# Relative bias of the MoBA scores added by VectorE from a skewed table, and two heads' scores ahead of the last mixer tile

## The reference

```python
own_pos = q_blk * BLK + blk_ar
bias_own = rel_bias[:, rel_bucket(q_pos[:, None] - own_pos[None, :])]
s_own = jnp.einsum('bhqd,bhkd->bhqk', q_c, k_own).astype(f32) + bias_own.astype(f32)[None]
s_own = jnp.where(own_pos[None, :] <= q_pos[:, None], s_own, -jnp.inf)
...
probs = jax.nn.softmax(logits, axis=-1).astype(v.dtype)
```

## Time and profile before

| what | us |
|---|---|
| three timed executions | 2479.95, 2473.61, 2477.56 |
| their median | 2477.56 |
| profiled execution, first to last instruction (span) | 2475.7 |
| median less that span | 1.9 |
| TensorE busy in the span | 2411.7 (97%) |
| VectorE busy | 1606.0 (65%) |
| ScalarE busy | 1033.3 (42%) |
| mean granted clock of TensorE | 0.994 of full speed |

### The profile page before, as it was taken

How to read it: one execution, slowest core, us unless ns; L and a number is a source line. 1 busy time by engine, 2 the same in 40 slices (tenths; PEclk the granted TensorE clock), 3 DMA queues, 4 the chain that set the end, 5 groups by cost and what they waited for, 6 DMA issues and landing times. The chain is left out here.

```text
span 2475.7 us, 41693 instructions
## 1 busy us (share of the span) xinstructions
PE 2411.7 (97%) x17447; PEld 2055.0 (83%) x17447; DVE 1606.0 (65%) x2242; ACT 1033.3 (42%) x1365; POOL 99.2 (4%) x179
## 2 busy tenths in 40 slices
PE   7999999999999999999999999999999999998999
PEld 7999989999999999899999854464888887647999
DVE  6887756778888887657798632671744442474555
ACT  5445534454554455335454321661422222263333
POOL 2010000001101100000001000000000000000000
PEclk9999999999999999999999999999999999999999
DMA  8776503647777775116467742102532331212452
GB/s 283 251 271 216 168 3 120 205 145 267 252 254 239 272 244 160 46 54 213 162 229 255 272 155 68 52 2 71 167 102 90 98 102 52 81 56 69 162 195 69
DMA packets 270807, 381.97 MB, mean 154 GB/s; under 512 B 9593, under 2 KB 235209, under 8 KB 268994
## 3 DMA queue, kind: packets, MB, share of 16 engines
q1 hardware_dynamic: 251628, 314.47, 38.7%
q0 software_dynamic: 18128, 64.20, 7.2%
q10 hardware_dynamic: 902, 1.15, 0.2%
HBM read 366.13 MB, written 13.65 MB: 153 GB/s over the span
## 5 line engine op out<-in xcount | busy, mean ns | idle before, releaser
L704 PE MATMUL ps<-span 128*128 128x512 f32 x1280 | 453.9, 399 | 2.3 <-issue 1.2
L635 PE MATMUL ps<-span,w_low 128*128 128x256 f32 x1440 | 408.0, 283 | 0.0
L706 PE MATMUL ps<-span,w_low 128*128 128x256 f32 x1280 | 359.5, 281 | 0.0
L633 PE MATMUL ps<-span 128*128 128x256 f32 x1216 | 348.6, 287 | 8.2 <-DVE span L1585 5.2
L1603 DVE TENSOR_TENSOR w_low<-ring,span 128x2048 fp32r<-128x2048 f32 x131 | 299.8, 2288 | 82.3 <-ACT span L1267 82.3
L1267 ACT ACTIVATE span<-ring 128x2048 fp32r<-128x2048 f32 x131 | 250.6, 1915 | 135.5 <-DMA ring<-in_ffn_w_in 112.8
L704 PEld LDWEIGHTS ps<-span 128*128 128x128 f32 x1280 | 240.6, 188 | 60.3 <-issue 1.3
L635 PEld LDWEIGHTS ps<-span,w_low 128*128 128x128 f32 x1440 | 277.0, 192 | 0.0
L634 PE MATMUL ps<-span 128*128 128x256 f32 x864 | 245.3, 284 | 0.0
L633 PEld LDWEIGHTS ps<-span 128*128 128x128 f32 x1216 | 233.8, 192 | 12.4 <-DVE w_low L1603 5.4
L706 PEld LDWEIGHTS ps<-span,w_low 128*128 128x128 f32 x1280 | 241.9, 189 | 0.0
(11 more groups left out here) (487 smaller groups left out, 5337.3 us busy)
## 6 DMA issues: line engine op xcount, KB each, us to landing
ring<-in_ffn_w_in SPq DMA_DIRECT2D x88, 1024.0 KB, 8.9
ring<-in_w_mlp SPq DMA_DIRECT2D x64, 1024.0 KB, 5.3
wmod<-in_w_mod POOLq DMA_DIRECT2D x96, 512.0 KB, 6.8
ring<-in_ffn_w_out SPq DMA_DIRECT2D x44, 1024.0 KB, 5.2
ring<-in_w_mix_in SPq DMA_DIRECT2D x26, 1024.0 KB, 5.5
ring<-in_xattn_w_kv SPq DMA_DIRECT2D x16, 1024.0 KB, 5.4
mod_scratch<-mod_acc POOLq DMA_DIRECT2D x24, 512.0 KB, 6.2
ring<-mod_scratch SPq DMA_DIRECT2D x12, 1024.0 KB, 4.9
```

Of the source, the lines that this page charges most:

```text
L633: mm(dst, w_hi, x_hi, start=start, stop=False, **more)
L635: return mm(dst, w_lo, x_hi, start=False, stop=stop, **more)
L704: mm(ps[bank + m].rearrange("p (w t) -> p w t", w=2), hi[:, k, cols], span[:, :, k, :], start=(k == 0), stop=False, skip_group_check=True)
L706: last = mm(ps[bank + m][:, 0:T], lo[:, k, cols], h_high[:, k, :], start=False, stop=(k == KD - 1), skip_group_check=True)
```

## The change

It has three parts.

1. The bias leaves TensorE. L793, L795 and the constant `flip` are gone. `maxima(h)` is given the bias table and uses `tensor_tensor_reduce`: it adds the table to the scores in place in PSUM and keeps the largest sum. The exponentials read the same bank as before.
2. The table is `toep`, whose partition p is the row read backwards from `hank`'s start. GpSimd writes the 8 rows to memory 16 times (one DMA, 128 rows of 512), and reads the table with eight DMAs of 16 partitions.
3. The scores use the banks `MOBA_BANKS = (2, 3, 0, 1, 4, 5, 0, 1)`. Heads 0 and 1 are scored right behind the head sums, ahead of the last mixer tile. ScalarE's exponentials of heads 0 and 1 stand ahead of its copy of the last tile, with a wait for the end of that tile in front of them. The scores of a head now wait for an earlier head's exponentials from head 6 on.

```diff
 def scores(h):
-    pair, hb, bank = h // 2, (h % 2) * HD, ps[SCORE_BANKS[h % 4]]
-    if h >= 4:
+    pair, hb, bank = h // 2, (h % 2) * HD, ps[MOBA_BANKS[h]]
+    if h >= 6:
         pe.wait_ge(*sm_act.at(l, 2 * (h - 3)))
     hi = slice(hb, hb + HD)
-    mm(bank[:, 0:T], cst["flip"], hank[:, h, :], start=True, stop=False, ...)
-    mm(bank[:, T:T + P], cst["flip"], hank[:, h, P:T], start=False, stop=False, ...)
-    mm(bank[:, 0:T], mq[hi, pair, P:T], mk[hi, pair, :], start=False, stop=False, ...)
-    mm(bank[:, T:T + P], mq[hi, pair, 0:P], mk[hi, pair, 0:P], start=False, stop=True, ...)
+    mm(bank[:, 0:T], mq[hi, pair, P:T], mk[hi, pair, :], start=True, stop=True)
+    mm(bank[:, T:T + P], mq[hi, pair, 0:P], mk[hi, pair, 0:P], start=True, stop=True
+       ).then_inc(*sc_done.up())
...
+def attend(first, end):
+    if first == 0:
+        pe.wait_ge(*mix_evac.at(l, 10))
+        pe.wait_ge(*act_step.at(l, ACT_KK_STD))
+    else:
+        pe.wait_ge(*dve_step.at(l, DVE_FEATURES))
+        pe.wait_ge(*mix_evac.at(l, MIX_TILES - 1))
+    for h in range(first, end):
+        step(h)
...
                     head_sums(tmp, 0)
-            pe.wait_ge(*dve_step.at(l, DVE_FEATURES))
-            moba(l)
+                    attend = moba(l)
+                    attend(0, 2)
+            attend(2, NH + 3)
...
 # GpSimd
-pool.dma_start(scratch["bias"], bias_rows).then_inc(bias_stored.sem, 16)
+pool.dma_start(scratch["bias"], bias_rows.rearrange("h (o t) -> h o t", o=1).to_broadcast(
+    [NH, BIAS_ROWS, 2 * T])).then_inc(bias_stored.sem, 16)
 pool.wait_ge(bias_stored.sem, 16)
-pool.dma_start(hank[:, :, :], bass.AP(src.tensor, 0, [[1, P], [2 * T, NH], [1, T]])
+for p in range(0, P, BIAS_ROWS):
+    pool.dma_start(toep[p:p + BIAS_ROWS, :, :], bass.AP(
+        src.tensor, P - 1 - p, [[2 * T - 1, BIAS_ROWS], [BIAS_ROWS * 2 * T, NH], [1, T]])
...
 # ScalarE, in front of take() of a value tile
+if n == MIX_TILES - 1:
+    act.wait_ge(w_used[FIRST_AT[("mix_in", j)] % RING].sem, freed(FIRST_AT[("mix_in", j)], l) + 1)
+    exponential, turned = softmax(l, 0, 1.0, (T, P), MOBA_BANKS)
+    exponential(0)
+    exponential(1)
 take(l, ("mix_in", j), mix_bank(n), mv[:, :, (j - 11) * BLK:(j - 10) * BLK], mix_evac)
...
 # VectorE, maxima(h)
-v.tensor_reduce(smx[:, e, t:t + 1], ps[banks[e]][:, at:at + w], AX_X, ALU.max
-                ).then_inc(*sm_max.up())
+if biases:
+    v.tensor_tensor_reduce(bank[:, at:at + w], bank[:, at:at + w], biases(h, t), 1.0,
+                           -3.0e38, ALU.add, ALU.max, smx[:, e, t:t + 1]).then_inc(*sm_max.up())
```

More of the change, by code:

```diff
@@ L113, in constants @@
         "head_ones": f(r // HD == c // HD),
-        "flip": f(r + c == P - 1),
         "eye": f(j == t),
@@ L164 @@
 SCORE_BANKS = (0, 1, 4, 5)
+MOBA_BANKS = (2, 3, 0, 1, 4, 5, 0, 1)
+BIAS_ROWS = 16
+BIAS_READY = 16 + P // BIAS_ROWS * 16
 CROSS_BANKS = (0, 1, 5, 4)
@@ L270, in program @@
         store["v_loaded"] = [Signal(ctx, nc, f"v_loaded{s}") for s in range(RING2)]
-        scratch = {"bias": nc.dram_tensor("bias_scratch", (NH, 2 * T), F32).ap(),
+        scratch = {"bias": nc.dram_tensor("bias_scratch", (NH, BIAS_ROWS, 2 * T), F32).ap(),
                    "mod": nc.dram_tensor("mod_scratch", (DEPTH, P, 2, MODS * P), F32).ap()}
@@ L312, in build_first @@
         part("under_mem", [P, KD, T])
-        part("under_hank", [P, NH, T])
+        part("under_toep", [P, NH, T])
         g_low = part("g_low", [P, KD, T])
@@ L335, in build_first @@
     mem_sb = sb("mem_sb", [P, KD, T])
-    hank = sb("hank", [P, NH, T])
+    toep = sb("toep", [P, NH, T])
     mix_buf = sb("mix_buf", [P, RAW + 4 * T])
@@ L820, in out, with step @@
                 last.then_inc(*av_done.up())
[L822 to L825, removed]
+            def attend(first, end):
[7 more added lines that the diff above has]
+                    step(h)
+            def step(h):
                 if h < NH:
@@ L831, in moba @@
                     out(h - 3)
+            return attend
         def heads_of(e):
@@ L1344, in exponential @@
             def exponential(h):
-                e, g, bank = h % 4, base + h, ps[banks[h % 4]]
+                e, g, bank = h % 4, base + h, ps[banks[h % len(banks)]]
                 act.wait_ge(*sm_max.at(l, 3 * (g + 1)))
@@ L1469, in scalar_program @@
             col_high(l, KV0)
-            exponential, turned = softmax(l, 0, 1.0, (T, P), SCORE_BANKS)
-            for h in range(NH + 2):
+            for h in range(2, NH + 2):
                 if h < NH:
@@ L1751, in shift, with softmax @@
                                                b[:, m, 1:T + 1], ALU.mult, ALU.add), mixed)
-        def softmax(l, base, scale, widths, banks):
+        def softmax(l, base, scale, widths, banks, biases=None):
             def maxima(h):
-                e, g = h % 4, base + h
+                e, g, bank = h % 4, base + h, ps[banks[h % len(banks)]]
                 dve.wait_ge(*sc_done.at(l, g + 1))
@@ L1758, in maxima @@
                 for t, w in enumerate(widths):
-                    v.tensor_reduce(smx[:, e, t:t + 1], ps[banks[e]][:, at:at + w], AX_X, ALU.max
-                                    ).then_inc(*sm_max.up())
+                    if biases:
+                        v.tensor_tensor_reduce(bank[:, at:at + w], bank[:, at:at + w], biases(h, t), 1.0,
+                                               -3.0e38, ALU.add, ALU.max, smx[:, e, t:t + 1]).then_inc(*sm_max.up())
+                    else:
+                        v.tensor_reduce(smx[:, e, t:t + 1], bank[:, at:at + w], AX_X, ALU.max
+                                        ).then_inc(*sm_max.up())
                     at += w
@@ L1969, in vector_program @@
             step(l, v.memset(state[:, :, :], 0.0), seq_step)
-            maxima, weights = softmax(l, 0, 1.0, (T, P), SCORE_BANKS)
+            if l == 0:
+                dve.wait_ge(bias_stored.sem, BIAS_READY)
+            maxima, weights = softmax(l, 0, 1.0, (T, P), MOBA_BANKS, lambda h, t: toep[:, h, t * P:T])
             evac = moba_out(l)
```

2 lines of the change are left out of this document (1 added, 1 removed).

## The result

The changed kernel takes 2488.2 us (median of four executions, 2483.65 to 2489.97) against 2478.8 us for the kernel before on the same chip (four, 2473.61 to 2481.05). The ratio is 1.0043, 95% interval 1.0029 to 1.0057: it is slower by 0.43% (the two medians alone give 1.0038). The forecast was 2472.5 us, and 2481 at most.

The account below looks back on a forecast made before the run. TensorE, busy 97% of the span, was taken as the bound. Per layer 6.80 us of products plus 1.37 of old waits less 5.6 of new gave 2.6, 5.1 in both: 2475.7 - 5.1 = 2470.6, median 2472.5; range 2467 to 2481.

Parts of the forecast that it names:

- TensorE's clock falls in the new gap: Rival: behind the idle 2.4 us before head 2 the clock drops, costing 1.6 us a layer, 2475.7 in all; chance 0.08.
- Bias products off TensorE, 6.80 a layer: Attention on TensorE: eight heads each lose 0.85 us of bias products, 6.80 us a layer, all in the gapless stretch.
- Two heads ahead of the last tile, 1.70 us, "no work is saved": Heads 0 and 1 scored before the last mixer tile: the tile starts 1.70 us later and ends at 303.95.
- Early scores gain nothing, head 2 waits 2.4: TensorE idles 2.4 us before head 2, which starts at 306.3 against 306.35 before; only heads 2 to 7 collect, 5.1.
- The pair at 0.95: VectorE's two sum-with-maximum instructions for a head, start to start up to the negation: 0.95 us, between 0.81 and 1.14.
- pipelined case: VectorE's pair with each accumulator read adding only 0.08 us: 0.81 us, a gain of 3.3 us a layer.
- cheap pair's rival: Rival: VectorE's pair costs as little as the reductions, 0.65 to 0.75 us; 7.0 to 7.8 gained, 2470.2; chance 0.2.
- New waits behind: TensorE waits appearing after head 2 starts, before the transposes of heads 1, 3 and 6: 0.8, 1.15 and 0.7 us.
- Edits at nothing: ScalarE's weight tile, GpSimd's eight table reads (up to 7.5 us to issue), SP's later loads and the shorter constants' load: no cost.
- Behind the attention "the gain is kept": After the attention TensorE's list keeps its order and the loads follow, so the 2.6 us a layer survives.
- VectorE as the bound: Rival: the pair takes 1.84 us in all 16 heads and every transpose waits; +1.9 us a layer, 2481.4; chance 0.12.

Follow-up runs that it names:

- e2: Kernel before with only the new banks and order, heads 0 and 1 scored early, bias products kept on TensorE: 2488.12 us, ratio 1.0051.
- e11: Kernel before with one unread product in front of TensorE's wait for the last mixer tile's copy: 2475.67 us, ratio 0.9996.
- e9: Changed kernel with four unread products of 64 rows filling TensorE's gap in front of head 2: 2473.55 us, ratio 0.9995.
- e3: Changed kernel with ScalarE's copy of the last mixer tile moved ahead of the exponentials of heads 0 and 1: 2483.25 us, ratio 1.003.
- e4: Changed kernel with four unread products of 128x128 by 128x256 in TensorE's gap in front of head 2: 2473.52 us, ratio 0.9997.
- e8: e1 with three unread products of 64 rows and 128 columns ahead of each head's scores: 2476.88 us, ratio 0.9999.
- e6: e5 with two unread products, one before the wait for the last tile's copy, one before head 0's transposes: 2467.95 us, ratio 0.9965.
- e5: e3 with both halves of the next projection's first weight tile made earlier, on ScalarE and VectorE: 2478.27 us, ratio 1.0011.
- e1: Changed kernel with the old order and banks, so only the bias moves to VectorE: 2487.07 us, ratio 1.0044.
- e10: e6 with a third unread product, in front of the wait for head 6's weights: 2467.48 us, ratio 0.9964.

## Why the prediction was wrong

**The step that failed** is the rival "TensorE's clock falls in the new gap". The prediction named the mechanism and its place, and sized both numbers wrongly: a chance of 0.08 and a price of "0.41 x 4 = 1.6 us" a layer.

- *The price.* It was the cost of the stretch in which the earlier trace rows show a clock of 0.59, as if a fall always ended after 4 us. Behind the attention's gap the clock was down for some 20 us. From head 2 to the last copy that is 24.50 - 17.68 = 6.8 us a layer and not 1.6. What should have been asked is what all the work behind the gap costs at half clock, up to the end of the attention: a head without its bias takes 2.13 at full clock and took 3.88, so five heads are 8.75 more, less the waits of 1.6 us (0.36, 0.69, 0.52) that vanish beside so slow an engine: 7.2 by this estimate, 6.8 measured.
- *The chance.* The argument against was that "TensorE is dense up to the 2.4 us gap here, and fairly dense behind it". The trace before had a counterexample: the stretch of the earlier trace rows lies behind an idle time of just this length. Of the kernel before:

```profile
1453.26 0.42 PE L2526 MATMUL ps<-consts_sb,sqm 24*128 24x24 f32 x4 [0.84 <-DVE sqm L3163]
1456.14 8.37 PE L2705 MATMUL ps<-h_sb,ring 128*128 128x512 f32 x15 [2.45 <-ACT h_sb L2919]
```

  The prediction called this "a thin stretch with gaps" and did not set the length of the gap beside its own. A wait of 2.45 us is followed by a fall there, 0.6 us behind its end; a forecast wait of 2.4 us should have been given the same, with a chance over a half. Not certainty: in the same trace a wait of 2.76 us, up to 2284.57, kept the full clock, and in the twelve profiles together the wait of 2.45 goes with a fall in ten and not in e2 and e11. That the fall was short there (0.98 from 1460 on) and long here is shown but not explained: there TensorE ran full-array products of 512 columns, here short products, transposes and outputs. e2 and e9 only say that the count of rows is not what decides whether it falls.

The Trainium skill, TensorE: Matmul & The Clock Gate, "Why this matters for your kernels", advises against idle gaps between bursts of products because one takes the clock to its lower level, but it names only gaps longer than any forecast here. The traces agree that idle time brings the clock down and differ on how much it takes: 2.39 us in one piece, and in e3 0.78 and 0.61 in two, were enough, and the measurement decides.

**The other steps, in order.**

- *Bias products off TensorE, 6.80 a layer*: right. They are gone, and e4, at full clock, gains 3.75 us up to the first layer's last copy.
- *Two heads ahead of the last tile, 1.70 us, "no work is saved"*: wrong, to the change's favour. The two took 0.86 us together, side by side, and the tile ended 0.6 us sooner than forecast.
- *Early scores gain nothing, head 2 waits 2.4*: the wait is right, 2.39, released by the copy of `mv`. Head 2 is at 305.74 where 306.3 was forecast and 306.35 stood before, so the early scores gained 0.6 us after all.
- *The pair at 0.95*: 0.78. The main parts are 0.43 and 0.33 (0.42 and 0.28 were taken); of the two reads of 0.14 only the second costs anything, 0.11. By the prediction's own scale this is just under its pipelined case, 0.81, and just over the cheap pair's rival (0.65 to 0.75).
- *New waits behind*: with the pair at 0.78 they are smaller, as e4 shows: 0.36 in front of head 1's transposes (forecast 0.8), 0.69 at head 3's (1.15), 0.52 at head 6's (0.7). Their order, with head 3 behind `col_low` the longest, was right. In the changed kernel itself they vanish, since TensorE at half speed waits for nobody.
- *Edits at nothing*: right for the features (+0.10). GpSimd's eight reads take 4.21 us of issuing, under the 7.5 allowed; the last goes out 71 us before the table is used.
- *Behind the attention "the gain is kept"*: off by 1.44 in the first layer and 0.48 in the second, where the recurrence is longer, with TensorE idle 0.84 in front of L878:

```profile
344.89 0.81 PE L878 MATMUL ps<-sc,mk 64*64 64x64 f32 x18 [0.84 <-issue]
```

  From the last copy of `cat` to the recurrence's first sum into it the first layer takes 31.82 us before, 33.26 after, and in the other kernels 31.84 (e2), 31.93 (e8), 32.48 (e11), 32.65 (e4), 32.70 (e6), 32.72 (e3), 32.78 (e5), 33.01 (e9), 33.28 (e1), 33.47 (e10). That follows neither the order nor the bias nor the clock of the attention. TensorE waits there for nothing that the profile records; what it is stays open, at some 2 us of the whole.
- *VectorE as the bound*: did not come. VectorE is idle in front of five of the eight maxima of the first layer, and in e4, at full clock, still in front of three.

The forecast time was the sum of steps that were mostly right or priced too high, the recurrences apart, at a clock that the change itself takes away.

## What to carry to other kernels

Taking work off a dense engine is only a gain if no idle stretch takes its place at a spot where much short work follows: list every wait of TensorE that the change will leave, and where they are like those here, price all the work behind them at half clock. Read the clock column beside the busy share, and look in the trace before for a wait of the same length and what the clock did after it. When such a wait can't be closed, two to four cheap products that nobody reads, in front of it, are worth trying; and what feeds the waiting instruction (here a weight tile's two halves) can be moved ahead of it. And where two heads of 64 rows lie on different halves of the partitions, score them back to back with nothing of full height between: here the second one cost nothing.

## What the hardware did that was not expected

- A fall of the clock outlasts its cause by far. In the changed kernel, e1, e2 and e3 there are eight such stretches in the attention, two in each; seven last 20 to 24 us, one (e2's second layer) 7, nearly all of it with TensorE recorded as busy. In the kernel before, behind 2.45 us of idle, it was under 4. What ends such a stretch stays open.
- The edge is soft. The second block, the same program in all twelve profiles, has waits of TensorE that can be counted: a stretch at the lower clock begins in the wait or up to 2.1 us behind it in none of the twelve at the wait of 1.74 us, in two at 1.77, in nine at 2.17, in ten at 2.45, in nine at 2.76 and in all at 4.00. e5's two layers have the same waits to 0.01 us, and one kept the clock and the other lost it; a median over a dozen executions then lies between two kinds of execution, and one profile shows only one of them.
- Products of 64 rows on partitions 0 to 63 and on 64 to 127 run side by side when they follow each other directly: two heads' scores take 0.86 us together in the changed kernel and 0.73 in e1 (303.29 to 304.02), with one head at 0.85. In e8 dummies on partitions 0 to 63 stand in line with head 0's scores (304.03, then 304.15) and run beside head 1's (305.02 and 305.03). In the kernel before, with bias products of 128 rows between them, each head's took its full 0.85 (303.80 to 304.65, 305.50 to 306.35).
- VectorE's read of the accumulator, 0.14 us long, starts at the same time as the instruction behind it and costs nothing where that does not need the result; where it does, as the negation, it adds 0.11 us. Adding and taking the maximum in place in PSUM takes 0.43 us for 256 columns and 0.33 for 128, against 0.422 and 0.281 for the maximum alone.
